# Mix stages in pairs of heads and strips of 128 columns, with the conv half of the output added early

## What is computed

```python
h = rmsnorm(x, g_mix[l])
z = h @ w_mix_in[l]                       # 1024 -> 3*512 + 3*512 + 8
zb, zc, zv, zq, zk, zval, zf = jnp.split(z, SPLITS, axis=-1)
y_conv = zb * causal_depthwise_conv(zc * zv, w_conv[l])      # 3 taps
log_f = jax.nn.log_sigmoid(zf + b_f[l])                      # one gate per head
# 8 heads of 64; c = cumsum(log_f); queries in 4 blocks of 128
s = q @ k.T * 64 ** -0.5 + c[q] - c[k]    # causal, softmax, then @ v
y = concatenate([rmsnorm(y_conv, g_conv_out[l]), rmsnorm(y_att, g_att_out[l])])
x = x + y @ w_mix_out[l]
x = x + memory_cross_attention(rmsnorm(x, g_xattn[l]), rmsnorm(mem, g_mem[l]), ...)
```

## Time and profile before

| | us |
|---|---|
| median of 3 runs | 3368.96 (3368.8 to 3375.22) |
| profiled execution | 3371.08 |
| its span, first to last instruction | 3369.1 |
| mean granted TensorE clock | 0.947 |

### The profile page before, as it was taken

The page is one execution under the profiler, slowest core; times in us unless marked ns, Lnnn a source line. Parts: engine busy times, 40 slices in busy tenths (PEclk is TensorE's granted clock), DMA queues, the critical chain, the costliest instruction groups (busy, mean ns, idle before and its releaser), DMA issues.

```text
span 3369.1 us, 36498 instructions
## 1 busy us (share of the span) xinstructions
PE 3105.9 (92%) x14928; PEld 2544.5 (76%) x14928; DVE 1601.5 (48%) x2406; ACT 1087.2 (32%) x1734; POOL 784.9 (23%) x436
## 2 busy tenths in 40 slices
PE   8999989798999999999899888999997898868898
PEld 6888867577888888888776677888876676656777
DVE  4553254543455434553356533555335455436663
ACT  3322243333333222322233333332222332333342
POOL 1000323253200000000322443100043444244432
PEclk8999999899999999999999899999997998879999
DMA  3332312032233233323211132323221111111111
GB/s 128 94 100 91 92 51 63 19 125 86 78 100 94 95 100 95 99 92 100 73 51 57 63 100 69 100 94 100 91 86 44 44 45 38 33 56 57 51 50 50
DMA packets 268838, 257.25 MB, mean 76 GB/s; under 512 B 10599, under 2 KB 267520, under 8 KB 268672
## 3 DMA queue, kind: packets, MB, share of 16 engines
q1 hardware_dynamic: 268416, 254.89, 24.0%
q0 software_dynamic: 256, 0.03, 0.0%
HBM read 252.79 MB, written 2.10 MB: 76 GB/s over the span
## 4 chain that ended last, share of the span: by engine, by line
PE 78%; DVE 11%; ACT 5%; POOL 2%; issue 2%; DMA 1%; SPq 0%; ACTq 0%; DVEq 0%; POOLq 0%
PE PS L1258 25%; PE PS L1259 24%; PE PS L1260 24%; PE PS L1264 2%; ACT WH L1627 1%; PE PS L1346 1%; ACT SC L1772 1%; POOL WL L2444 1%; PE PS L1407 1%; DVE AF L2351 1%; DVE AR L2082 1%; DVE SM L2123 1%; PE PS L1394 1%; DVE AR L2167 1%; DVE AR L2098 1%
## 5 line engine op out<-in xcount | busy, mean ns | idle before, releaser
L1258 PE MATMUL PS<-XH,WL 128*128 128x512 f32 x2256 | 922.8, 409 | 28.0 <-DVE XL L1989 15.3
L1259 PE MATMUL PS<-XL,WH 128*128 128x512 f32 x2256 | 896.2, 397 | 0.0
L1260 PE MATMUL PS<-XH,WH 128*128 128x512 f32 x2256 | 896.2, 397 | 0.0
L1627 ACT ACTIVATE WH<-RAW 128x1024 fp32r<-128x1024 f32 x448 | 465.5, 1044 | 1043.0 <-PE PS L1260 1015.5
L1981 DVE TENSOR_TENSOR WL<-RAW,WH 128x1024 fp32r<-128x1024 f32 (+1 forms) x296 | 367.1, 1241 | 601.9 <-ACT WH L1627 545.5
L2444 POOL TENSOR_TENSOR WL<-RAW,WH 128x1024 fp32r<-128x1024 f32 (+1 forms) x186 | 446.2, 2405 | 753.3 <-ACT WH L1627 723.8
L1258 PEld LDWEIGHTS PS<-XH,WL 128*128 128x128 f32 x2256 | 434.3, 192 | 112.1 <-DVE XL L1989 15.7
L1258 PE MATMUL PS<-AR,WL 128*128 128x512 f32 (+1 forms) x1216 | 474.8, 390 | 43.5 <-DVE SC L2076 24.4
L1260 PEld LDWEIGHTS PS<-XH,WH 128*128 128x128 f32 x2256 | 433.6, 192 | 94.6
L1259 PEld LDWEIGHTS PS<-XL,WH 128*128 128x128 f32 x2256 | 435.2, 193 | 79.8 <-issue 1.9
L1259 PE MATMUL PS<-AR,WH 128*128 128x512 f32 (+1 forms) x1216 | 468.3, 385 | 0.0
(11 more groups left out here) (246 smaller groups left out, 3561.5 us busy)
## 6 DMA issues: line engine op xcount, KB each, us to landing
RAW<-in_w_ffn_gu_dram SPq DMA_DIRECT2D x176, 512.0 KB, 3.5
RAW<-in_w_ffn_down_dram SPq DMA_DIRECT2D x80, 512.0 KB, 3.3
RAW<-in_w_mix_in_dram SPq DMA_DIRECT2D x48, 512.0 KB, 3.6
RAW<-in_w_xkv_dram SPq DMA_DIRECT2D x32, 512.0 KB, 3.3
...
```

Of the source, the lines that this page charges most:

```text
L1258: pe.matmul(o, ll, rh, start=start, stop=False, skip_group_check=skip)
L1259: pe.matmul(o, lh, rl, start=False, stop=False, skip_group_check=skip)
L1260: return pe.matmul(o, lh, rh, start=False, stop=stop, skip_group_check=skip)
L1627: act.activation(h, src, ACT.Copy).then_inc(sg["wh"].up(n))
```

## The change

- Attention in mix goes by pairs of heads, 16 rows of two heads in a stage, with functions that sb and mix now share. `ms` makes six score products by turns in the two halves of the array, one key-bias product per head, and two masks. The key bias has 40 rows per head: the high parts of the 8 heads at rows 0 to 7 of a half, the low parts at rows 32 to 39, in one tile NC of 104 partitions; for this zf is computed in four copies. One reduce serves both heads. The normalising multiply goes from DVE to POOL (`mn`).
- q, k, zc, zv, zb come in strips of 128 columns, in another order; v stays in chunks of 256. After the barrier come the forget chain, v0 and zc0, then `ctr`.
- Intermediates of the conv are kept in PSUM and CB. `cbl`, `mpl`, `btl`, `mn` and others are put off by a given amount of TensorE work (`later`, `due`, `tick`).
- In the output projection all eight half tiles of the conv come first, woven with the last attention rows; `evc` multiplies each and adds it to X. `mem_a` comes behind the fourth, `mem_b` behind the eighth. Then come the eight half tiles of the attention with `eva`.
- In all stages, `low` and `scale` are due by a clock of TensorE steps (`PACE`) instead of list entries. In `split`, the low part of unit n-3 is written first if it is still open.
- Small: eight transfers instead of two for b_f, one for the table E8.

```diff
+PACE = {"mm": 1, "vmm": 0.5, "score": 1, "dscore": 1, "tr": 0.5, "bs": 1.5, "ms": 2, "bt": 1, "bpv": 2.5, "mpv": 2.5, "dpv": 2, "xpv": 2}
...
-        if kind not in ("load", "split", "low", "scale"):
-            while self.halves and self.halves[0][1] <= len(self.order):
+        if kind in PACE:
+            self.clock += PACE[kind]
+            while self.halves and self.halves[0][1] <= self.clock:
                 self.low()
-            while self.scales and self.scales[0][1] <= len(self.order):
+            while self.scales and self.scales[0][1] <= self.clock:
                 self.scale()
...
                 w, wo = a["w_mix_in"][l], a["w_mix_out"][l]
+                def heads(t):
+                    self.strip((s, f"q{t}"), w, 3 * CW + t * 128)
+                    self.strip((s, f"k{t}"), w, 4 * CW + t * 128)
+
+                heads(0)
+                self.unit(((s, "zf"), 0), w[:, 6 * CW:6 * CW + 8].rearrange("(k p) c -> p k c", p=128), kind="pad")
                 self.cols((s, "v0"), w, 5 * CW)
+                for m in range(4):
+                    if m == 3:
                         self.cols((s, "v1"), w, 5 * CW + 256)
+                    self.strip((s, f"zc{m}"), w, CW + m * 128)
+                    self.strip((s, f"zv{m}"), w, 2 * CW + m * 128)
+                    self.strip((s, f"zb{m}"), w, m * 128)
+                    if m < 3:
+                        heads(m + 1)
+                for u in range(2):
+                    for p in range(4):
+                        src = wo[u * 512:u * 512 + 512, p * 256:p * 256 + 256].rearrange("(k p) c -> p k c", p=128)
+                        self.unit(((s, f"o{p}"), u), src)
+                    for r in range(0 if u else 2):
+                        self.unit(("mem", s, r), a["mem"][0, r * 128:(r + 1) * 128, :].rearrange("p (k c) -> p k c", c=128), kind="mem")
+                continue
...
-                    self.scales.append((n, len(self.order) + 6))
+                    self.scales.append((n, self.clock + 6))
...
+                    self.ready(n - NRAW)
...
-                    self.halves.append((n, len(self.order) + 4))
+                    self.halves.append((n, self.clock + 4))
...
+        def qk(w, t):
+            b = self.take()
+            yield from self.tile(((s, f"{w}{t}"), 0), b)
+            self.give(b)
+            self.heads_in(s, w, t)
+
+        def conv(w, m):
+            b = self.take()
+            yield from self.tile(((s, f"z{w}{m}"), 0), b)
+            self.give(b)
+            if w == "c":
+                self.add("cc", (s, m), "cc")
+            elif w == "v":
+                self.add("cv0", (s, m))
+                self.add("cv1", (s, m), "cv")
+                for i, step in enumerate(("cv2", "cv3", "cv4")):
+                    self.later(2 * i + 2, step, (s, m))
+            else:
+                for step in ("cv2", "cv3", "cv4"):
+                    self.due(step, (s, m))
+                self.add("cb0", (s, m))
+                self.add("cb1", (s, m), "cy")
+                self.add("cb2", (s, m), "csq", *(("cacc",) if m else ()), "yh")
+                self.later(4, "cbl", (s, m), "yl")
+
...
+        def att(n0, n1):
+            for n in range(n0, n1):
+                m = n - 2
+                if m > 0 and m % 4 == 0:
+                    self.due("btl", (s, m - 1))
+                    for i in range(2):
+                        self.due("evl", (((s, f"v{(m - 4) // 8}"), 0), i))
+                    for hh in range(2):
+                        values_of(m // 4 - 1, hh)
+                        yield
+                if 0 <= m < 16:
+                    self.due("mn", (s, m))
+                    self.due("btl", (s, m - 1))
+                    self.add("bt", (s, m), "ptr", "ph")
+                    self.later(4, "btl", (s, m), "pl")
+                    yield
+                if n < 16:
+                    for w in "qk":
+                        self.due("bql", (s, w, n // 4))
+                    self.due("mn", (s, n - 1))
+                    self.add("ms", (s, n), "score", "nbias", "exps")
+                    self.later(10, "mn", (s, n), "fac", "gprob")
+                    yield
...
+        def close(m, u):
+            self.give(self.chunks[(s, f"o{m // 2}"), 4 * u].banks[m % 2])
+            if u == 0:
+                self.add("evc", (s, m), "oc")
+            else:
+                self.add("eva", (s, m), "x", at=(s + 1, m))
...
+        self.add("forget", (s,), "z8", "fgz", "fgl", "cum", "nch", "ncl")
+        self.drain(self.flow(self.values(s, 0)))
+        self.drain(self.flow(conv("c", 0)))
+        self.add("ctr", (s,), "ctr", "cq")
+        side = self.stream(att(0, 4), 6.5 / 64)
+        self.weave(self.flow(self.chain(conv("v", 0), conv("b", 0), qk("q", 1), qk("k", 1))), side)
+        for m in (1, 2):
+            self.finish(side)
+            side = self.stream(att(4 * m, 4 * m + 4), 10.5 / 80)
+            self.weave(self.flow(self.chain(conv("c", m), conv("v", m), conv("b", m), qk("q", m + 1), qk("k", m + 1))), side)
+        side = self.stream(att(12, 16), 10.5 / 80)
+        self.weave(self.flow(self.chain(self.values(s, 1), conv("c", 3), conv("v", 3), conv("b", 3))), side)
+        self.own_banks(0, 1, 2, 3, 4, 5)
+        side = self.stream(att(16, 19), 4.5 / 40)
+        for m in range(8):
+            self.weave(self.flow(half(m, 0)), side)
+            if m == 1:
+                ny_a(0)
+            elif m == 3:
+                ny_b(0)
+                for i in range(4):
+                    close(i, 0)
+                self.add("mem_a", (s,), "msq", "mms", "mpw", "mrow")
+            elif m > 3:
+                close(m, 0)
+        self.finish(side)
+        self.tick(99)
...
+        self.own_banks(0, 1, 2, 3, 4, 5, 6, 7)
+        for m in range(8):
+            self.drain(half(m, 1))
+            if m == 1:
+                ny_a(1)
+            elif m == 3:
+                ny_b(1)
+                for i in (0, 1):
+                    close(i, 1)
+                self.post(s + 1, (0, 1))
+            elif m > 4 and m % 2:
+                for i in (m - 3, m - 2):
+                    close(i, 1)
+                self.post(s + 1, (m - 3, m - 2))
+        for i in (6, 7):
+            close(i, 1)
...
+    def later(self, wait, *step, **at):
+        self.soon.append([wait, step, at])
+    def due(self, *step):
+        for x in list(self.soon):
+            if x[1][:2] == step:
+                self.soon.remove(x)
+                self.add(*x[1], **x[2])
+    def tick(self, n=1):
+        for x in list(self.soon):
+            x[0] -= n
+            if x[0] <= 0:
+                self.soon.remove(x)
+                self.add(*x[1], **x[2])
+        self.watch(n)
+    def flow(self, g):
+        for n in g:
+            self.tick(n)
+            yield n
...
+            def ms(s, n):
+                N = pair_scores(s, n)
+                on.wait_ge(*sg["mask"].at(s))
+                on.wait_ge(*sg["ncl"].at(s))
+                for hh in range(2):
+                    h = 2 * (n // 4) + hh
+                    r = slice(64 * hh, 64 * hh + 40)
+                    pe.matmul(PS[4 + hh][:, 0:N], EH[r, h:h + 1].to_broadcast([40, 128]), NC[r, 0:N], start=False, stop=False)
+                pair_masks(s, N).then_inc(sg["score"].up(s, n))
+                free[4] = free[5] = [sg["exps"].at(s, n)]
+
...
+                for hh in range(2):
+                    m = 2 * (n % 2) + hh
+                    e = act.activation(PM[n % 2][:, hh, 0:N], PS[4 + hh][:, 0:N], ACT.Exp, bias=NB[:, hh:hh + 1], accum_out=LS4[:, m:m + 1])
+                e.then_inc(sg["exps"].up(s, n))
...
+            def ms(s, n):
+                t, i = divmod(n, 4)
+                N = 128 * (i + 1)
+                on.wait_ge(*sg["score"].at(s, n))
+                dve.reduce_max(MX, PSUM[:, 4:6, 0:N], AX).then_inc(me.up())
+                on.wait_ge(*me.last())
+                on.wait_ge(*sg["cq"].at(s))
+                for hh in range(2):
+                    q = CQ[:, i, 2 * t + hh:2 * t + hh + 1]
+                    b = dve.scalar_tensor_tensor(NB[:, hh:hh + 1], MX[:, hh:hh + 1], q, q, ALU.add, ALU.subtract, reverse1=True)
+                b.then_inc(sg["nbias"].up(s, n))
+
+            def mn(s, n):
+                p = slice(2 * (n % 2), 2 * (n % 2) + 2)
+                on.wait_ge(*sg["exps"].at(s, n))
+                dve.reciprocal(RL4[:, p], LS4[:, p]).then_inc(sg["fac"].up(s, n))
 
             def score(s, r):
...
+            def half_in(s, m, u, g):
+                ch = ((s, f"o{m // 2}"), 4 * u)
+                o = PS[chunks[ch].banks[m % 2]][:, :]
+                on.wait_ge(*sg["mm"].at(ch, m % 2, 3))
+                on.wait_ge(*sg["yr"].at(s, u))
+                dve.tensor_tensor(o, o, RY[u], ALU.mult).then_inc(me.up())
                 on.wait_ge(*me.last())
+                dve.tensor_tensor(X[:, m, :], X[:, m, :], o, ALU.add).then_inc(g)
+            def evc(s, m):
```

(9 more changed lines are left out.)

721 lines of the change are left out of this document (311 added, 410 removed).

## The result

| | before | after |
|---|---|---|
| median of 4 runs, us | 3368.88 (3367.84 to 3375.22) | 3242.28 (3238.06 to 3246.95) |
| profiled execution, span, us | 3369.1 | 3236.0 |
| mean granted clock | 0.947 | 0.962 |

The account below looks back on a forecast made before the run. TensorE's work, waits and clock were taken to bound the kernel (78% of the chain is TensorE). 3371.1 less 55 (mix_0), 57 (mix_1), 4 (x) and 17.7 (sb) gives 3237.4; less 2.1 for a median run, 3235; range 3190 to 3300.

Parts of the forecast that it names:

- Products of the scores: Mix attention: a pair of heads costs 1.40 us at 512 keys and 0.86 at 128, saving 25 us a mix.
- changes of shape: Mix: 16 score groups and 16 transpose groups fewer, at about 0.12 us each, save 4 us a mix.
- The lower bound taken for the key bias: Pair scores: both heads' key-bias products overlap and cost one product, 0.23 us at 512 keys and 0.10 at 128.
- Waits: Mix: about 33 us of TensorE waits go and 12 us of new ones come, each mix; bounds 0 and 33.
- the early conv half: Mix output projection: eight half tiles, 21.8 us of products, cover the waits of 9.6, 5.2 and 5.9 us.
- The pair chain: Mix pair rows: scores to transposes takes 7 to 9.5 us, covered by about 10.8 us of TensorE products.
- rival E: Slower: multiplies queue on POOL behind two low parts, 5.5 us wait in each of 32 rows, 3411 us; chance 0.03.
- The x stages: Start of x_0 and x_1: 2 us less wait each, as last tiles close with fewer adds, 4 in all.
- The start of sb: End of diff into sb: the second norm product comes 17.7 us earlier; bounds 0 and 19.2.
- What the pace does elsewhere: Outside mix, due times in PE steps change nothing in full ffn stages but bring sb's second norm product 17.7 us earlier.
- The median: Whole kernel: a median run is 2.1 us below the profiled execution's 3237.4, so 3235 us.
- rival C: All cover holds: new waits 3 instead of 12 a mix, clock fully up, fewer shape changes, 3209 us; chance 0.15.

Follow-up runs that it names:

- The two exchanges of the pace: Old pace of low parts and scales in the changed kernel: 3252.52 us, ratio 0.9645; new pace alone in the kernel before: 3353.58 us, ratio 0.9949.
- the changed kernel once more: The changed kernel run again with nothing changed: 3242.36 us, ratio 0.9612; diff took 482.5 us instead of 475.6.

## Why the prediction was right, and where it wasn't

A mix stage comes apart into three terms: TensorE's waits, what the granted clock cost in its busy time (half of the busy time that passed at the lower of its two levels), and the rest, its products at full clock.

| us | mix_0 before | after | change | forecast | mix_1 change |
|---|---|---|---|---|---|
| products at full clock | 262.7 | 235.1 | -27.6 | -29 | -26.8 |
| waits | 34.0 | 11.1 | -22.9 | -21 | -22.3 |
| clock | 11.9 | 6.1 | -5.7 | -6 | -9.8 |

So the sum for the mix stages was right term by term, and not by luck.

**Products of the scores: right.** A pair costs 1.41 and 0.87 us at 512 and 128 keys against 1.40 and 0.86. Over all four lengths the timeline has 2.63 us for two heads before and 1.10 for a pair after, 24.6 us a stage for the forecast 25. That leaves 3.0 of the 27.6 for the changes of shape, forecast 4. The lower bound taken for the key bias was the true one; doubling it shows the same price again.

**Waits: right in the sum and in most members.** 34.0 went, 11.1 came; 12 was forecast, with 3.3 (3.7 measured), 2.3 (2.3), 1.0 (1.4), 1.5 (1.1, and 2.9 in mix_1) and 4 for small ones at the pair rows (2.6, none of it for a transposed pair). That the forget chain needs its cover is shown: without it 13.6 us of wait come back, of a chain that is 13.8 by the rows of before (8.4 of wait and 5.4 of products). With it the scan ends 4.0 us before the transposes need it.

What the early conv half is worth, however, had been put too high by the earlier trace rows: with the old order in the new kernel only the wait for mem's transposes returns, and it costs 9 to 10 us a mix. The 5.9 behind the conv stay away. Whether the shorter conv code or the shorter attention does that wasn't tried apart, and no run has single heads or chunks of 256 columns in the new kernel.

**The pair chain: covered, but tight where the rows are long.** In mix_0, from the end of the scores to the end of the multiply, it takes 4.1 to 10.6 us (forecast 7 to 9.5), and the transposes come 7.8 to 21.6 us after the scores (forecast 10.8 for all). The two tightest rows, with 512 keys, need 8.4 of 10.5 us. The multiply itself is shorter than in sb, 0.6 to 1.9 us where the forecast had 0.7 to 2.8. Doubling it adds 1.9 us to these rows and leaves 0.1 us, so the stages grow by 3 us only; rival E needed 4.2 us of wait in every row to be slower than before. The rule of the Trainium skill on VectorE and GpSimd ("SBUF — State Buffer", § Who interferes with whom) doesn't decide this: moved back, the multiply costs 3 us more. It does agree with the operation of one element in the earlier trace rows, of which the prediction read only the mean of 491 ns: the median of its 32 is 220 ns and the longest 2195, and the 22 that have GpSimd idle beside them take 219 to 221. It also agrees with the tail of mix_0, where two low parts of X on VectorE (two inputs in SBUF) take 1.6 us while GpSimd stands and 3.6 beside its low part and sum, here in VectorE's timeline:

```profile
633.36 1.63 DVE L2069 SCALAR_TENSOR_TENSOR XL<-X,GA,XH 128x512 fp32r<-128x512 f32 x2
...
637.57 3.65 DVE L2069 SCALAR_TENSOR_TENSOR XL<-X,GA,XH 128x512 fp32r<-128x512 f32 x2
```

**The x stages: wrong.** The step that failed is "The stage x behind each starts with 2 us less wait, since the last tiles are closed with fewer adds". It counted operations per tile and not tiles: four are closed behind the last product instead of two. In x_0 the low part of v0 was in GpSimd's queue behind all of their sums, because under the new pace the many entries of a closing no longer count (7.3 us; old pace: gone); in x_1 the fourth product wanted a bank that the last tile held (7.8 us; tiles closed earlier: gone). The two stages took 7.7 us more instead of 4 less. The new pace alone costs 3.1 and 3.2 us there, in the kernel before; the prediction had put that at nothing, since it followed GpSimd's queue at the start of sb and not at the start of x.

**The start of sb: right in its mechanism, too small in its size.** The second norm product came 27.1 us after the end of diff, forecast 25.3, which is 16.0 less than before (forecast 17.7); the first came 16.8 earlier (forecast 19). The chain has the order that was laid out (start, us, what):

```profile
2870.61 2.31 POOL WL L2536
2872.92 3.77 issue
2876.72 1.90 POOL RAW L2522
2878.62 0.99 POOL SM L2558
...
2880.12 0.66 PE PS L1339 x4
```

The other 11.7 us of the 27.7 come in the attention rows of sb, in steps of 1.5 to 4 us at the second row of all groups of four but the first, and the third row gives some of it back. The sum had nothing for them: "What the pace does elsewhere" looked at the start of the stage only. The two exchanges of the pace show that it is the cause, and that VectorE is busy 15 us less; what makes the steps stays open.

**The median: 7 us off.** The profile was forecast at 3237.4 and measured at 3238.1, but that it came within 1 us is luck: +11.7 in x and -10 in sb cancel. That the median would be 2.1 below the profiled execution failed: here it lies 4 above. The clock in diff is the likely cause, as in the changed kernel once more, but no trace shows it for the other executions. The range was safe by far; how its lower end, 3190, follows from rival C's 3209 the prediction doesn't show.
